# Three transformer blocks in one kernel: seven-product multiplication for seven more input slots, and the third mixer's key norm by logarithm and exponential

## The reference, cut to what matters

```
# second block, state-space branch: 512 channels of B and C for every 4 groups, from the normed input
bc = silu(causal_conv4(h @ w_in[:, bc_columns], conv_w, conv_b))
# third block
proj = rmsnorm(x) @ w_in
rw = proj[..., D_NSA_IN:]                     # 14 tiles of 128 channels
rw = rw + (token_shift(rw) - rw) * rwkv_mu
r, k, v, xw, xa, xg = split(rw)
kk = heads(k * k_k)
kk = kk / maximum(sqrt(sum(kk * kk, axis=-1)), 1e-12)
k_cmp = rmsnorm(gelu(windows(kc) @ cmp_w1 + b1) @ cmp_w2 + b2)   # windows of compressed keys, values alike
bonus = sum(rh * kh * r_k, axis=-1) * vh
```

## Time and profile before

| What | us |
| --- | --- |
| median of three runs | 3539.42 |
| lowest and highest of them | 3539.38, 3542.52 |
| the profiled execution's own time | 3544.15 |
| span of the profiled execution, first to last instruction | 3542.3 |
| TensorE busy | 3508.7 (99%) |
| VectorE busy | 1631.7 (46%) |
| GpSimd busy | 1586.8 (45%) |
| ScalarE busy | 771.6 (22%) |

### The profile page before, as it was taken

The page is one execution under the profiler, slowest core; times in us unless marked ns, Lnnn a source line. Parts: engine busy times, 40 slices in busy tenths (PEclk is TensorE's granted clock), DMA queues, the critical chain, the costliest instruction groups (busy, mean ns, idle before and its releaser), DMA issues.

```text
span 3542.3 us, 47135 instructions
## 1 busy us (share of the span) xinstructions
PE 3508.7 (99%) x19513; PEld 2898.6 (82%) x19513; DVE 1631.7 (46%) x2588; ACT 771.6 (22%) x1409; POOL 1586.8 (45%) x1322
## 2 busy tenths in 40 slices
PE   8999999999999999999999999999999999999999
PEld 7888888688888888867888888888887458678888
DVE  3221222533336322136746633688622475378851
ACT  2000142332111100013444300100012455320000
POOL 4454312005355455417885664366640122136653
PEclk9999999999999999999999999999999999999999
DMA  4322333423332333232323222233223410033322
GB/s 138 84 84 86 84 68 72 81 58 66 72 76 91 84 84 92 79 101 84 107 96 102 84 84 95 84 84 85 88 89 105 84 36 6 6 84 93 86 84 71
DMA packets 369368, 286.39 MB, mean 81 GB/s; under 512 B 10259, under 2 KB 359059, under 8 KB 369156
## 3 DMA queue, kind: packets, MB, share of 16 engines
q1 hardware_dynamic: 366852, 279.44, 28.7%
q10 hardware_dynamic: 2304, 3.95, 0.4%
HBM read 280.64 MB, written 2.72 MB: 80 GB/s over the span
## 4 chain that ended last, share of the span: by engine, by line
PE 97%; ACT 1%; DVE 1%; issue 1%; POOL 0%; DMA 0%; SPq 0%; DVEq 0%; POOLq 0%; ACTq 0%
PE psum L618 44%; PE psum L1092 25%; PE psum L1058 3%; PE psum L3605 2%; PE psum L1781 2%; PE psum L1495 2%; PE psum L2516 2%; PE psum L4198 1%; PE psum L587 1%; PE psum L3700 1%; PE psum L1768 1%; PE psum L4472 1%; PE psum L3563 1%; PE psum L1747 1%; PE psum L1640 1%
## 5 line engine op out<-in xcount | busy, mean ns | idle before, releaser
L618 PE MATMUL psum<-work 128*128 128x256 f32 (+1 forms) x2400 | 551.4, 381 | 0.0
L537 POOL TENSOR_TENSOR work<-weight_ring 128x512 f32<-128x512 f32 x132 | 163.5, 1239 | 785.2 <-PE psum L618 728.7
L618 PEld LDWEIGHTS psum<-work 128*128 128x128 f32 x2400 | 456.0, 190 | 66.0
L618 PE MATMUL psum<-work,weight_ring 128*128 128x256 f32 (+1 forms) x2080 | 481.8, 381 | 0.0
L618 PE MATMUL psum<-normalized,weight_ring 128*128 128x256 f32 (+1 forms) x2016 | 468.2, 382 | 2.7 <-DVE normalized L738 2.7
L618 PEld LDWEIGHTS psum<-work,weight_ring 128*128 128x128 f32 x2080 | 395.2, 190 | 57.2
L618 PEld LDWEIGHTS psum<-normalized,weight_ring 128*128 128x128 f32 x2016 | 383.7, 190 | 61.1 <-DVE normalized L738 4.2
L762 DVE TENSOR_TENSOR work<-work,psum 128x512 f32<-128x512 f32 (+1 forms) x100 | 68.7, 686 | 641.1 <-PE psum L618 641.1
L1092 PE MATMUL psum<-work 128*128 128x256 f32 x1424 | 331.9, 379 | 0.0
L1092 PE MATMUL psum<-work,weight_ring 128*128 128x256 f32 x1344 | 314.4, 379 | 0.0
L1000 POOL TENSOR_TENSOR work<-weight_ring 128x512 f32<-128x512 f32 x74 | 95.8, 1295 | 476.9 <-PE psum L1092 343.8
(11 more groups left out here) (565 smaller groups left out, 5110.7 us busy)
## 6 DMA issues: line engine op xcount, KB each, us to landing
weight_ring<-in_w_in SPq DMA_DIRECT2D x72, 1024.0 KB, 7.0
weight_ring<-in_w_ffn_in SPq DMA_DIRECT2D x88, 512.0 KB, 5.1
weight_ring<-in_ffn_w_up SPq DMA_DIRECT2D x44, 512.0 KB, 4.7
weight_ring<-in_ffn_up SPq DMA_DIRECT2D x44, 512.0 KB, 5.1
weight_ring<-in_w_ffn_out SPq DMA_DIRECT2D x16, 1024.0 KB, 4.9
weight_ring<-in_w_out SPq DMA_DIRECT2D x12, 1024.0 KB, 5.0
work<-decay_sums SPq DMA_DIRECT2D x16, 512.0 KB, 4.6
weight_ring<-in_w_proj_b SPq DMA_DIRECT2D x8, 1024.0 KB, 5.0
```

Source lines behind the costliest of these rows:

```text
L537: own(pool.tensor_tensor(s1, a21, a22, ALU.add))
L618: last = pe.matmul(K.ps[:, self.BANK[m] * T:self.BANK[m] * T + self.H], left(m, p), right(pe, m, p), start=first and p == 0, stop=last_par ...
```

## The change

In the second mixer, the plan `bc` of four slots becomes `bc_first`, two slots as whole tiles, and `bc`, two slots as seven products (`self.early`), ahead of the others. GpSimd's sums of the input and of these weights move ahead of its first state-space work, and the small transposes `times_pe` come one tile sooner.

In the third mixer, the first five of the seven slots become seven products (`self.inputs`), in PSUM banks 4 to 7; the last two stay whole (`rwkv_rest`). The sums of the input need room, so ScalarE's queue stores the residual (2 MB) in device memory, the sums take its place, and SyncE's queue brings it back after the fifth slot. The evictions go to SBUF (`self.raws`), from which ScalarE and VectorE then read. The compressed hidden layer has its operands swapped: windows stationary (62 columns), weights moving (128 columns), the two kinds alternating between array columns 0 and 64, and two transposes more (`turn_hidden_pe`). The head sums of keys and bonus now share bank 3, so `bonus_pe(t)` waits for `kk_rooted(t + 2)`. The key norm becomes: maximum with 1e-24 by VectorE out of PSUM, then Ln and Exp with factor -0.5 by ScalarE, and no reciprocal.

```diff
-    ORDER = (("bc", 8),)
+    ORDER = (("bc_first", 4),)
+    EARLY = 2
...
+        early_sums_at = [[self.xs + (3 * n + i) * T for i in range(3)] for n in range(self.EARLY)]
+        self.early = Sevens(K, [plans["bc"]], banks, early_sums_at, parts)
+        self.side = Sevens(K, [plans[name] for name in ("xs", "gmlp_u", "gmlp_v")], banks, self.side_sums_at, parts, after=self.early,
+                           by_token=[plans["gmlp_v"]])
...
-        for c in self.whole_tiles_pe(pe, "bc"):
-            if c == 3:
+        for c in self.whole_tiles_pe(pe, "bc_first"):
+            if c == 2:
                 self.times_pe(pe)
+        for j in range(self.EARLY):
+            for _ in self.early.job_pe(pe, j, self.u_side, self.early_side_pe if j == 0 else lambda pe, m, p: None):
+                pass
         self.spent = 0
         side = self.side_pe(pe)
         for g in range(SSM_GROUPS):
-            self.side_until(side, 5 * (g + 1))
+            self.side_until(side, 8 + 5 * g)
...
+        pool.wait_ge(*S["ended"](1))
+        self.u_side.first_sums(pool, own, 0, KD // 2).then_inc(S["u_summed"].h, 1)
+        G, E = self.side, self.early
+        E.sums_pool(pool, 0)
+        pool.wait_ge(*self.plans["bc_first"].done(1))
+        self.u_side.last_sum(pool, 0, KD // 2).then_inc(S["u_summed"].h, 1)
+        E.sums_pool(pool, 1)
         pool.wait_ge(*S["by_token"](1))
...
+        for j in range(self.EARLY):
+            self.early.three_into_dve(dve, j, K.bank(4, HALF_BANK))
+            self.early.five_into_dve(dve, j, K.bank(5, HALF_BANK, P, HALF_BANK))
+            self.early.all_into_dve(dve, j, self.raw_others())
+            self.taps_dve(dve, own, j)
...
+RWKV_SEVENS = 5
...
+        v, bonus, ar = self.v, self.bonus, self.ar
+        places = [(v, v + T, v + 2 * T), (v + 3 * T, bonus + 2 * T, bonus + 3 * T)]
+        self.raws = ar + 2 * T
+        self.inputs = Sevens(K, [plans["rwkv_in"]], (4, 5, 6, 7), [places[n % 2] for n in range(RWKV_SEVENS)],
+                             [ar + 6 * T + i * HALF_BANK for i in range(4)])
+        self.u_side = ApartHalves(U, KD * TM, 0, TM, X, lambda i, p: i * 2 * T + p * HALF_BANK)
...
-        sp.wait_ge(*S["hidden"](2))
+        sp.wait_ge(*S["hidden"](1))
...
+        self.weights(sp, "rwkv_rest")
         self.weights(sp, "w_out3")
+        sp.wait_ge(*S["rw_ready"](2 * RWKV_SEVENS))
+        sp.dma_start(self.tokens_of_x(), by(self.store, T)).then_inc(S["x_back"].h, 16)
...
-        pool.wait_ge(*S["hidden"](2))
+        own, D = self.K.own_pool.of(pool), self.inputs
+        pool.wait_ge(*self.norm.scaled(KD))
+        pool.wait_ge(*S["x_stored"](16))
+        self.u_side.first_sums(pool, own, 0, KD // 2).then_inc(S["u_summed"].h, 1)
+        self.u_side.last_sum(pool, 0, KD // 2).then_inc(S["u_summed"].h, 1)
+        for n in range(3):
+            D.sums_pool(pool, n)
+        pool.wait_ge(*S["hidden"](1))
         pool.memset(A(self.ks, 4 * T), 0.0).then_inc(S["k_cleared"].h, 1)
+        D.sums_pool(pool, 3)
...
+            if t == 0:
+                self.inputs.sums_pool(pool, 4)
...
-        self.rwkv_tile_pe(pe, 4)
+        self.turn_hidden_pe(pe)
+        job = self.rwkv_job_pe(pe, 2)
+        for _ in range(14):
+            next(job)
         self.lora_pe(pe, 0)
-        self.rwkv_tile_pe(pe, 5)
+        for _ in job:
+            pass
         self.second_pe(pe)
         self.kk_sum_pe(pe, 0)
         self.lora_pe(pe, 1)
         self.rwkv_slot_pe(pe, 3)
         self.kk_sum_pe(pe, 1)
         self.turn_kc_pe(pe)
+        self.lora_pe(pe, 2)
         self.bonus_pe(pe, 0)
-        self.lora_pe(pe, 2)
         self.rwkv_slot_pe(pe, 4)
         self.kk_sum_pe(pe, 2)
+        self.lora_pe(pe, 3)
         self.bonus_pe(pe, 1)
-        self.lora_pe(pe, 3)
         self.rwkv_slot_pe(pe, 5)
         self.kk_sum_pe(pe, 3)
+        self.rwkv_tile_pe(pe, 12)
         self.bonus_pe(pe, 2)
-        self.rwkv_slot_pe(pe, 6)
+        self.rwkv_tile_pe(pe, 13)
         self.bonus_pe(pe, 3)
...
     def rwkv_slot_pe(self, pe, k):
-        for n in (2 * k, 2 * k + 1):
-            self.rwkv_tile_pe(pe, n)
+        if k < RWKV_SEVENS:
+            for _ in self.rwkv_job_pe(pe, k):
+                pass
+        else:
+            for n in (2 * k, 2 * k + 1):
+                self.rwkv_tile_pe(pe, n)
+
+    def rwkv_job_pe(self, pe, j):
+        S = self.s
+
+        def ready(pe, m, p):
+            if p == 0 and m == 1:
+                pe.wait_ge(*S["q_squared"](4))
+            elif p == 0 and m == 5:
+                pe.wait_ge(*S["kv_copied"](2))
+            elif p == 0 and m in (6, 7):
+                pe.wait_ge(*S["u_summed"](1 if m == 6 else 2))
+        return self.inputs.job_pe(pe, j, self.u_side, ready if j == 0 else lambda pe, m, p: None)
...
+        pe.wait_ge(*S["windows"](4))
+        pe.wait_ge(*S["q_ready"](4))
+        for kk in range(KK):
+            for i in range(2):
+                last = pe.matmul(K.bank(3, P)[self.by_window(i)], A(self.win + (i * KK + kk) * 2 * CMP, 2 * CMP),
+                                 A(self.w1 + (i * KK + kk) * P, P), start=kk == 0, stop=kk == KK - 1, skip_group_check=True)
+        last.then_inc(S["hidden"].h, 1)
...
         pe.wait_ge(*S["kk_squared"](t + 1))
         if t == 0:
-            pe.wait_ge(*S["kv_copied"](2))
+            pe.wait_ge(*S["activated"](2))
+        elif t > 1:
+            pe.wait_ge(*S["bonus_copied"](t - 1))
         else:
-            pe.wait_ge(*S["kk_rooted"](t))
-        pe.matmul(K.bank(7), K.head_ones[:, :], self.feature_buffers(t)["sq"], start=True, stop=True).then_inc(S["kk_summed"].h, 1)
+            pe.wait_ge(*S["kk_rooted"](1))
+        pe.matmul(K.bank(3), K.head_ones[:, :], self.feature_buffers(t)["sq"], start=True, stop=True).then_inc(S["kk_summed"].h, 1)
 
     def bonus_pe(self, pe, t):
         K, S = self.K, self.s
         pe.wait_ge(*S["t1_ready"](t + 1))
-        if t == 0:
-            pe.wait_ge(*S["activated"](2))
-        elif t == 1:
-            pe.wait_ge(*S["kc_ready"](2))
-            pe.wait_ge(*S["vbd_ready"](8))
+        if t < RWKV_TILES - 1:
+            pe.wait_ge(*S["kk_rooted"](t + 2))
         else:
-            pe.wait_ge(*S["bonus_copied"](t - 1))
-        pe.matmul(K.bank(3 - t % 2), K.head_ones[:, :], self.feature_buffers(t)["t1"], start=True, stop=True)\
+            pe.wait_ge(*S["bonus_copied"](t))
+        pe.matmul(K.bank(3), K.head_ones[:, :], self.feature_buffers(t)["t1"], start=True, stop=True)\
             .then_inc(S["bonus_summed"].h, 1)
...
+        act.wait_ge(*self.norm.settled(KD))
+        act.dma_start(by(self.store, T), self.tokens_of_x()).then_inc(S["x_stored"].h, 16)
...
-        act.wait_ge(*S["kk_summed"](t + 1))
-        act.activation(f["sq"], self.K.bank(7), ACT.Sqrt).then_inc(S["kk_rooted"].h, 1)
+        own = self.K.own_act.of(act)
+        act.wait_ge(*S["kk_guarded"](t + 1))
+        own(act.activation(f["sq"], f["sq"], ACT.Ln))
+        own.wait()
+        act.activation(f["sq"], f["sq"], ACT.Exp, scale=-0.5).then_inc(S["kk_rooted"].h, 1)
 
...
+        if k < RWKV_SEVENS:
+            D, H, raw = self.inputs, HALF_BANK, self.raws
+            if k:
+                dve.wait_ge(*S["rw_ready"](2 * k))
+            D.three_into_dve(dve, k, A(raw, H))
+            D.five_into_dve(dve, k, A(raw + 3 * H, H))
+            D.all_into_dve(dve, k, by(A(raw + H, 2 * H), H))
...
-            dve.wait_ge(*S["bonus_summed"](t))
             dve.wait_ge(*S["features"](t))
         own(dve.tensor_scalar(f["k2"], f["a"], -1.0, V("k_a_3")(t), ALU.add, ALU.mult))
+        dve.wait_ge(*S["kk_summed"](t + 1))
+        dve.tensor_scalar(f["sq"], self.K.bank(3), 1e-24, None, ALU.max).then_inc(S["kk_guarded"].h, 1)
+        own.wait()
+        own(dve.scalar_tensor_tensor(out=f["k2"], in0=f["k2"], scalar=1.0, in1=k, op0=ALU.add, op1=ALU.mult))
+        own.wait()
+        if t:
+            dve.wait_ge(*S["bonus_summed"](t))
+        dve.scalar_tensor_tensor(out=f["t1"], in0=r, scalar=V("r_k_3")(t), in1=f["k2"], op0=ALU.mult, op1=ALU.mult)\
+           .then_inc(S["t1_ready"].h, 1)
         dve.wait_ge(*S["kk_rooted"](t + 1))
-        own(dve.tensor_scalar(f["sq"], f["sq"], 1e-12, None, ALU.max))
-        own.wait()
-        own(dve.reciprocal(f["sq"], f["sq"]))
-        own(dve.scalar_tensor_tensor(out=f["k2"], in0=f["k2"], scalar=1.0, in1=k, op0=ALU.add, op1=ALU.mult))
-        own.wait()
         dve.scalar_tensor_tensor(out=f["kk"], in0=k, scalar=V("k_k_3")(t), in1=f["sq"], op0=ALU.mult, op1=ALU.mult)\
            .then_inc(S["kk_ready"].h, 1)
-        dve.scalar_tensor_tensor(out=f["t1"], in0=r, scalar=V("r_k_3")(t), in1=f["k2"], op0=ALU.mult, op1=ALU.mult)\
-           .then_inc(S["t1_ready"].h, 1)
         dve.wait_ge(*S["kk_ready"](t + 1))
         dve.wait_ge(*S["exps"](t + 1))
         dve.scalar_tensor_tensor(out=self.chunks_of(t, 0), in0=by(f["kk"], CHUNK), scalar=-1.0, in1=by(f["sg"], CHUNK), op0=ALU.mult,
```

(25 more changed lines are left out.)

151 lines of the change are left out of this document (87 added, 64 removed).

## The result

The changed kernel takes 3548.78 us (median of 9 runs, 3547.69 to 3552.24), the kernel before 3541.38 (9 runs); the ratio is 1.0022, 95% interval 1.0014 to 1.0030. That is 7.4 us slower, inside the range given, but 3 us beyond the forecast of +4.5, and just over the 0.2% that was called the bound of what can be told. The forecast time, 3543.9, is 4.9 short: 2.9 of it is the change's, and 2.0 is the kernel before, which stood at 3539.42 in its first three runs.

What follows compares the result with a forecast made beforehand. TensorE, busy for 99% of the span, was taken to bound the kernel. Terms -12.3 - 2.7 + 16.1 + 3.4 = +4.5 us on the median of 3539.42 gave 3543.9 us, range 3533 to 3552.

Steps and rivals of the forecast that it cites:

- Seven products: Second and third mixer: seven slots as seven products each gain 1.76 us of TensorE, 12.3 us in all.
- Sums hidden: Both mixers: the sums behind the seven products cost nothing; no TensorE idle time for them.
- Hidden layer: Third mixer's compressed hidden layer: swapped operands in overlapping column halves take 4.2 us, not 7.25; minus 2.7 with two more transposes.
- Waits: Third mixer: TensorE waits 1.2 us at turn_kc_pe, 9.0 at bonus_pe(0), 5.9 at bonus_pe(1); plus 16.1.
- Clock: Third mixer: TensorE's clock falls in the two bonus_pe waits, half speed afterwards costing 1.7 us each; plus 3.4.
- Ln, table load, Exp: Key norm's root on ScalarE: a 1.28 us table load stands between Ln and Exp; without it the sum is 2.6 lower.
- Rival 1: Third mixer: waits as computed, but the clock hardly falls; sum +1.1, 3540.5 us; chance 0.15.
- Rival 2: Third mixer: waits mostly covered, only 2 us left in all; sum -13, 3526.4 us; chance 0.12.
- Rival 3: Chain to the root: VectorE and GpSimd slow one another at two shifts and the maximum; sum +10, 3549.4 us; chance 0.18.

Runs made afterwards that it cites:

- halves: Changed kernel with the hidden layer's loops exchanged, all 16 matmuls into the lower column half, then 16 into the upper; 3554.01 us in one execution.
- guarded: Changed kernel with bonus_pe(t) and kk_sum_pe(1) waiting for VectorE's maximum (kk_guarded) in place of ScalarE's root; 3542.75 us, ratio 1.0005.
- apart: Changed kernel with bonus sums in bank 2, head sums alone in bank 3, compressed key turned later, no wait for the root at bonus_pe; 3530.62 us, ratio 0.9971.

## Why the forecast was near, point by point

- **Seven products, -12.3.** Measured -11.3, and -10.6 with what was lost beside it: this term was 1.7 us too good and is the largest part of the miss in the first profile. A slot gains 1.64 in the second mixer and 1.54 to 1.65 in the third, not 1.76, since a slot goes to the next operation's start in 12.08 to 12.19 (12.48 for slot 2, cut in two), and I had taken 12.08 against the longer of the whole slots (13.84; others take 13.73). In the second mixer 3.3 of gain became 2.55: TensorE waits 0.50 at the second group's products, the wait that I had bounded by 0 and 1 and taken as 0. It waits for ScalarE's copy of the first group's product (L2851), which stands behind the SiLU of a convolved tile. The other 0.2 was not traced.

```profile
1628.17 0.46 PE L2668 MATMUL psum<-work 128*128 128x128 f32 x2 [0.50 <-ACT work L2851]
```

- **Sums hidden.** Right: no wait at L1093 in either mixer of the changed kernel.
- **Hidden layer, -2.7.** Measured -3.1 (from L3703's start to slot 2: 4.87, before 7.97). 3.71 us and not 4.2; the run halves shows that the overlap of rows 4 was the right reason.
- **Waits, +16.1.** Measured 16.05: 1.73, 8.38 and 5.94 against 1.2, 9.0 and 5.9. A longer wait at `turn_kc_pe` leaves a shorter one at `bonus_pe(0)`: the two are 10.1 together and were forecast at 10.2, so the mechanism and the chain's length are right and not only the sum. The runs guarded and apart show that they come from the shared bank and the turned key, with 2.2 of other waits behind them.
- **Clock, +3.4.** The other part of the miss, 0.5 to 1.7 us. Measured 3.9 in the first profile, 4.1 and 5.1 in the two others. The working was right, half of the time at low clock; I had 3.4 us of work in each low stretch, and there were 3.5 to 5.4. My upper bound was 3.4 of cost for each fall, 6.8 in all, and the value chosen inside it was too low.
- **Added up:** -11.3 + 0.7 - 3.1 + 16.05 + 3.9 to 5.1 = +6.3 to 7.5. The two stretches show 6.2 and 7.35 directly, the medians 7.4 (interval 5 to 10.6). The forecast's +4.5 was short by 1.7 of products and 0.5 to 1.7 of clock, and the hidden layer gave 0.4 back.
- **Ln, table load, Exp.** The load of 1.28 stands there in each root, as in the list. By the rule of the Trainium skill ("ScalarE: Activation LUTs", section "Table sets: the hidden batching unit") it would not be there; here the trace speaks against it. The prediction put two such loads, 2.6 us, on TensorE's path. There are three, since the root of features 0 stands ahead of `turn_kc_pe` (VectorE waits 0.90 for it in the changed kernel): without them the waits would be some 3.8 shorter, an estimate.
- **Rival 1** (clock hardly falls) is wrong, 0.50 is granted. **Rival 2** (waits covered) is wrong. **Rival 3** has its mechanism (1.23 for 0.16), but at another place than I gave: slot 4's sums ended at 2807.3, the shifts began at 2808.28, so the shifts stayed at 0.70 each. What paid was a copy and a scale, with one SBUF input each, where I had looked at operations with two. The maximum out of PSUM kept 0.69 beside a GpSimd product (2811.11, the product from 2810.90 to 2812.32).
- The chances leaned on a sum of +4.5. A sum of +6.9, the middle of the +6.3 to 7.5 above, would have put slower and same about even; that the measured 0.22% lies just over the bound of 0.2% says little for or against them.
